# A short product of zeros in front of each float32r unit, and the g buffers at another distance from the weight slots

## The reference

```python
merged = g_s5 * (y_s5 @ w_br_s5[l]) + g_m * (y_m @ w_br_m[l])
x = x + merged @ w_out[l]
x = x + _cross_attn(h, _rmsnorm(mem, mem_norm_g[l]), x_wq[l], x_wkv[l], x_wo[l])
x = x + _conv_ffn(h, f_w_up[l], f_conv_w[l], f_conv_b[l], f_w_down[l])   # first block
...
y = even_mixer(...) if l % 2 == 0 else odd_mixer(...)                    # second block, twice
x = layer_norm(alpha * x + y, ln_g[l, 0], ln_b[l, 0])
y = conv_ffn(x, ffn_w_up[l], ffn_conv_w[l], ffn_conv_b[l], ffn_w_down[l])
x = layer_norm(alpha * x + y, ln_g[l, 1], ln_b[l, 1])
```

## Time and profile before

| | us |
|---|---|
| median of 3 runs | 1260.06 |
| lowest, highest | 1257.33, 1261.47 |
| profiled execution, its own time | 1257.58 |
| span of the profiled execution | 1256.3 |
| TensorE products busy | 1214.3 (97% of the span) |
| weight loads busy | 1115.8 (89%) |
| VectorE busy | 901.3 (72%) |
| ScalarE busy | 610.2 (49%) |

### The profile page before, as it was taken

One profiled execution on the slowest core, in us unless ns is written; L12 is line 12 of the kernel. 1 busy time (PEld: TensorE's weight loads), 2 busy tenths in 40 slices (PEclk: granted clock), 3 DMA queues, 4 the chain that ended last, 5 costly groups with the idle time before them and its releaser, 6 DMA issues. The chain is left out here.

```text
span 1256.3 us, 21189 instructions
## 1 busy us (share of the span) xinstructions
PE 1214.3 (97%) x8528; PEld 1115.8 (89%) x8528; DVE 901.3 (72%) x1266; ACT 610.2 (49%) x919; POOL 108.0 (9%) x148
## 2 busy tenths in 40 slices
PE   8999999989999999999998999999998999999997
PEld 5888888988999999989988899999986898999996
DVE  5977996574768888855678767767665689666677
ACT  2252213453656666644664545655414554655552
POOL 3893000003000000010000000000200000000000
PEclk9999999998999999999999999999999899999999
DMA  9543444535734766625425356667455205556560
GB/s 275 178 152 114 134 135 135 184 108 158 239 134 168 234 213 224 204 75 160 127 89 189 135 183 220 225 219 184 101 153 162 68 1 169 189 180 201 189 213 36
DMA packets 178734, 202.76 MB, mean 161 GB/s; under 512 B 21884, under 2 KB 163163, under 8 KB 178636
## 3 DMA queue, kind: packets, MB, share of 16 engines
q1 hardware_dynamic: 175083, 191.49, 47.9%
q0 software_dynamic: 3184, 9.77, 2.7%
q10 hardware_dynamic: 369, 0.13, 0.1%
HBM read 200.30 MB, written 1.08 MB: 160 GB/s over the span
## 5 line engine op out<-in xcount | busy, mean ns | idle before, releaser
L1483 DVE TENSOR_TENSOR w_parts<-raw,w_parts 128x1024 fp32r<-128x1024 f32 (+1 forms) x242 | 294.9, 1219 | 125.1 <-ACT w_parts L1472 119.8
L1766 PEld LDWEIGHTS ps<-hT_parts,w_parts 128*128 128x128 f32 x2880 | 338.5, 189 | 2.3
L1766 PE MATMUL ps<-hT_parts,w_parts 128*128 128x256 f32 x2880 | 340.3, 279 | 0.0
L1472 ACT CAST w_parts<-raw 128x1024 fp32r<-128x1024 f32 (+1 forms) x242 | 253.6, 1048 | 159.1 <-PE ps L1766 59.9
L478 PE MATMUL ps<-hT,ring 128*128 128x256 f32 x448 | 100.3, 384 | 1.2 <-DVE hT L321 1.2
L1536 PE MATMUL ps<-hT_parts,w_parts 128*128 128x256 f32 x816 | 98.5, 281 | 2.1 <-DVE w_parts L1483 1.5
L1536 PEld LDWEIGHTS ps<-hT_parts,w_parts 128*128 128x128 f32 x816 | 96.2, 189 | 2.9 <-DVE w_parts L1483 1.7
L478 PEld LDWEIGHTS ps<-hT,ring 128*128 128x128 f32 x448 | 85.7, 193 | 14.4 <-issue 1.6
L1890 DVE SCALAR_TENSOR_TENSOR arena_late<-ps,vecT,arena_late 128x255 f32<-128x255 f32 (+1 forms) x176 | 84.9, 482 | 10.3 <-ACT arena_late L1840 4.0
L1785 PE MATMUL ps<-w_parts,g0T_parts 128*128 128x512 f32 x360 | 86.7, 396 | 1.1 <-DVE w_parts L1483 1.1
L1785 PE MATMUL ps<-w_parts,g1T_parts 128*128 128x512 f32 x360 | 84.8, 390 | 0.0
(11 more groups left out here) (417 smaller groups left out, 1608.3 us busy)
## 6 DMA issues: line engine op xcount, KB each, us to landing
raw<-in_ffn_w_up SPq DMA_DIRECT2D x44, 1024.0 KB, 5.1
raw<-in_f_w_up SPq DMA_DIRECT2D x22, 1024.0 KB, 5.2
raw<-in_ffn_w_down SPq DMA_DIRECT2D x22, 1024.0 KB, 5.0
ring<-in_w_in SPq DMA_DIRECT2D x18, 1024.0 KB, 5.9
raw<-in_ev_w_in SPq DMA_DIRECT2D x15, 1024.0 KB, 5.4
raw<-in_f_w_down SPq DMA_DIRECT2D x11, 1024.0 KB, 5.0
ring<-in_x_wkv SPq DMA_DIRECT2D x8, 1024.0 KB, 5.4
ring<-in_w_out SPq DMA_DIRECT2D x4, 1024.0 KB, 8.2
```

Source lines behind the costliest of these rows:

```text
L1472: self.done(A, A.copy(high[:, c], self.raw[:, u % RAW, c]), self.s_hi)
L1483: self.done(V, V.tensor_tensor(low[:, c], self.raw[:, u % RAW, c], high[:, c].bitcast(F32), ALU.subtract), self.s_lo)
L1766: mm = T.matmul(self.ps[:, b, m * 256:m * 256 + 256], w[:, kk, m * P:(m + 1) * P], x[:, kk, :], start=kk == 0 and q == 0, stop=kk == KD - ...
```

## The change

Each unit of parts, and each PSUM bank of it where it has several, gets one product in front: 128 x 128 bfloat16 zeros as the stationary operand, 64 columns of zeros as the moving one. It writes columns 0 to 63 of the bank that the unit's first real product then overwrites. In `pe_up` a unit that is issued in two halves gets it before the first half alone. The pads around the g buffers change from 192 and 128 bytes to 320 and none: g0 moves up by 128 bytes, g1 and everything behind it stay where they are.

```diff
@@ pe_unit
             self.take(b)
+            if u in self.split1:
+                self.pe_short(b)
             for j in range(2):
@@ pe_out1
                 self.take(b)
+                self.pe_short(b)
                 for kk in range(KD):
@@
+    def pe_short(self, b):
+
+        self.T.matmul(self.ps[:, b, 0:64], self.zb[:, 0:P], self.zb[:, 0:64], start=True, stop=True)
@@ late_memory
-        for i, pad in enumerate((3, 2)):
-            self.sb(f"pad_g{i}", [P, pad * LINE])
+        for i, pad in enumerate((5, 0)):
+            if pad:
+                self.sb(f"pad_g{i}", [P, pad * LINE])
             self.gTr.append(self.sb(f"g{i}T_parts", [P, 2, 2, SEQ], F32R))
@@ pe_late
             self.take(b)
+            if split:
+                self.pe_short(b)
@@ pe_up
         self.take(b)
+        if half != 1:
+            self.pe_short(b)
```

## The result

| | before | after |
|---|---|---|
| median, us | 1260.76 (4 runs) | 1270.82 (4 runs) |
| lowest, highest | 1257.33, 1262.02 | 1267.6, 1272.37 |
| profiled execution: span | 1256.3 | 1269.5 |
| units with weights stationary, long pace | 2472 of 3936 products | 1368 of 3936 |
| units with weights moving, long pace | 735 of 864 | 492 of 864 |

The ratio is 1.0081 with a 95% interval of 1.0058 to 1.0103: 10 us slower, where the forecast was +0.2 us. The time lies inside the wide range (1251 to 1275) and outside the forecast's own (1256 to 1265). The last two rows of the table are counted from the timelines, stretch by stretch, in the way that the prediction counted.

A forecast was written before the change was run, and what follows sets the result against it. TensorE's stream of products was taken to bound the kernel: 13.1 us for zeros, less 11.0 from the pace and 1.9 from g0, made +0.2, put on the median as 1260.3 us; own range 1256 to 1265, wide range 1251 to 1275.

The forecast's parts named there:

- long pace: TensorE's 512-column products in some stretches: 118 ns from start to start, counted for 2472 of 3936 weights-stationary products.
- rival (a): All 118 starts: the zeros don't reset the pace, and units fall into the long pace; +17.7 us, 1277.8 us; chance 0.20.
- What bounds the kernel: Feed-forward networks: TensorE's products alone form the chain, so a nanosecond per product moves the end one for one.
- The price: All 118 products of zeros: 0.12 us each for an exposed weight load, less 1.1 us; 13.1 us, bounds 3.5 and 16.5.
- Rival (b): Products of zeros: cheap, only 0.03 us each, if loads could run two ahead; -9.4 us, 1250.7 us; chance 0.13.
- g0's move: Down units on g0: moving the buffer by 128 bytes brings 86.7 us to 84.8, worth 1.9 us.
- Nothing else differs: Down units on g0 against g1: position alone explains 86.7 against 84.8 us, so the move is worth 1.9 us.
- short pace: TensorE's 512-column products in the other stretches: 113 ns from start to start, counted for 1464 of 3936 weights-stationary products.
- The return: Weights-stationary units: all 2472 products at the long pace go to the short one, 11.0 us saved.
- 15 in 18 exposed starts: Weights-stationary units whose first weight load was exposed: 15 of 18 take the short pace, used to convert 2472 products.
- rival (c): Weights-moving units: another 735 products take the short pace too, 3.3 us; total -3.1 us, 1257.0 us; chance 0.17.
- The queues hold nothing new: DMA queues across the kernel: nothing else comes late, so they got no term in the sum.

## Why the prediction was right or wrong

The time fell into the wide range, but not for the reasons given. The forecast's own range ends at 1265, slower by more than 0.3% had a chance of 0.23, and the measured 1270.8 lies between the forecast and rival (a). Two things made the difference: the return was less than half of what was counted, and a stage that had no term in the sum grew. That the wide range covered the second one as well is luck.

**What bounds the kernel** held. In the networks each product of zeros is paid in full on the chain, and nothing hides it. No wait on VectorE appeared ahead of the up units.

**The price** held: 0.13 to 0.14 us for the 0.12 taken; 118 x 0.14 - 1.1 = 15.4 us at most for 13.1. The ground for it held too. The first real load begins with the product of zeros (both loads start together in the timeline of PEld, at 1104.03 and 1104.02, as the product of zeros does). Rival (b) is out, and the Trainium skill's issue floor of about 25 ns for products of up to 64 columns (TensorE: Matmul & The Clock Gate, Back-to-back issue gap) is not what such a product costs here. Beside float32r loads the first one costs 0.13 us; the second one in a row, at 0.03 to 0.04, is near it.

**g0's move** held in itself (1.6 us for 1.9), and failed in what it was taken to leave alone. The step "Nothing else differs" is wrong: a down unit at an odd multiple of 128 bytes gives the units behind it the short pace, and at a multiple of 256 the long one (but for the first down unit of a network, which leaves the long one in every trace without a second product of zeros). The prediction had this row before it (short pace behind g0 in 9 of 9 cases) and treated it only as a bound, on the ground that the zeros would reset the pace. In its trace the move alone costs 1.9 us in the networks.

**The return** is the step that failed: "every weights-stationary unit now begins behind a short product with a bare load", so all 2472 products would take the short pace. In net 1104 did: 1104 x 4.45 ns = 4.9 us for 11.0. 1152 of the remaining 1368 are 24 units, the first up unit behind each of the eight down units a network that have up units behind them. Fifteen of them had the long pace before and kept it; nine, behind g0, had the short one and lost it by the move of g0. There a single product of zeros changes nothing, as the experiment with zeros alone shows on both kinds of down unit; between two up units it does set the short pace. The count of 15 in 18 exposed starts came from starts behind transposes, attention groups and waits, with several short products or an idle array ahead; it was carried over to a single short product directly behind 512-column ones, of which the trace had no case. Behind down units two in a row suffice. Two readings on the way were off as well. The row of 11.26 us is no stretch at the short pace: (11.26 - 0.28)/95 is 115.6 ns, and the trace has 48 of its products at 118 and 48 at 113, with no break between. So a pace can change without one, and what changed it there is open. And that every stream behind products of 256 float32 columns starts at the long pace has an exception in the same trace: the unit at 607.33 stands behind eight of them and is 5.72 us long. Of the weights-moving units 243 products converted, 1.1 us, about a third of rival (c).

The sum of units by these terms: 15.4 - 4.9 - 1.1 - 1.6 + 0.3 = +8.1 us with every zero at 0.14, +5.8 at 0.12. By stages, 3.8 us are seen in the networks and 1.4 in the first block; what is left would stand in the mixers' stages, where the stretches at half clock differ between the two traces by more than that, so it is not shown. For the networks alone the terms are 60 x 0.13 - 576 x 4.45 ns - 1.6 + 0.3 = +3.9, against 3.8 measured. So rival (a), which wanted more than half of the 60 up units at the long pace, didn't come: 24 of 60 have it. The kernel lies between it and the forecast, and 0.21 us to win for 0.12 to pay was too thin a margin for a part of the units to miss it.

**What was not in the sum** is the stage at 292 us, +3.1 and +6.6 us in two profiled executions. "The queues hold nothing new" was wrong: instructions added to TensorE add code, and code comes through the same DMA engines. That the wait at the `x_wq` load goes with the position of the code is seen in both directions, in one trace each: 17 more products at the start bring it to the kernel before, 111 more take it from the changed one; and of twelve traces the four with a block in this load are the four with a wait of more than 1 us. The product of zeros itself does nothing there, since with two for one the wait is absent. What it costs the median is not shown. The kernel before with its code shifted has a ratio of 1.0019, about 2 us, and a median only 0.6 us up; the changed kernel with its code shifted on has nearly the ratio of the changed one. The shifted kernel's two clusters lie 4 to 5 us apart, but only an execution of the upper one was traced, and the kernel with two products of zeros has such an upper cluster without the wait. So of the 10 us the units account for 5 to 8, by the stages and by the terms; this stage, the start and the clock share the rest.

Not settled: why 16 KB cost a 1 MB load 1.3 to 4.5 us. The share of q1 in the 5.2 us from the issue is no proof, since it is 78.3% with the block and 79.9% without it in the kernel with its code shifted on, where the load is as fast as before the change. The block took 1.7 us of one DMA engine's time in the changed kernel's trace (2.1% of 16 engines in 5.2 us), and the copies of `bias_rows` begin right where the load should end; a part of the load that is held up by the block would then meet them at a third of the rate. No trace speaks against this, and it was not tested; a kernel that issues these copies later would do that.

## What to carry to other kernels

A stream of products has more than one pace, and what one unit ends with can set the pace of the next. So a position of a buffer is to be judged by the unit behind it too, not only by the products that read it: here 1.9 us won in the down units cost 3.8 in the up units. A count of cases (15 of 18) holds for the situation in which they were counted; before it is multiplied by a thousand products, look whether one of the cases is the one that the change makes. When instructions are added to TensorE, ask which load its code blocks will now meet. A stage whose trace grows by 3 to 5 us without any new dependence in it can be code.

## What the runs showed of the hardware

- **The pace and 256 bytes.** A 512-column float32r product with its load takes 227 ns when g (here the stationary operand) and the weight slots (here the moving one) are a multiple of 256 bytes apart (512 and 768), 232 ns at odd multiples of 128 (640 and 896), whichever buffer it is: down units of 5.44 to 5.46 and 5.57 us. The Trainium skill (TensorE: Matmul & The Clock Gate, Step-by-step) gives the array separate read ports for weights and moving data, and by that the position would be of no account. Four positions say otherwise. That it is a conflict of reads is not shown.
- **What resets the pace.** Directly behind a 512-column down unit one 64-column product of zeros leaves the pace that this unit set (24 of 24 places); two in a row put it to the short one (24 of 24). Between two up units one is enough (33 of 33 in the changed kernel's trace). For units with weights moving neither holds: 492 of 864 products stay at the long pace behind one. Why is not known.
- **Code blocks.** TensorE's code comes in blocks of 16 KB, 68 to 70 of them here, on queue q8. The Trainium skill (Runtime: NRT & Kernel Launch, Instruction fetch mechanics) says the same of the size and calls the cost mostly hidden. For TensorE itself the traces agree. For this load, which is due at once, they don't: 5.2 to 5.8 us without a block in it, 6.5 to 9.7 with one, in four profiled executions of twelve.
- **The clock.** Stretches at half clock stand in every kernel's trace, near 12 to 35, 283 to 297 and 962 to 1014 us, and their total, without the last one, in which the work ends, differs from one execution to the next: 20.5 us in the trace of before, 24 to 27 in most others, 31 to 34 in three. The first 17 us of before's trace are 1.6 to 2.2 us shorter than in eight of the others, 0.3 shorter than in one and 3.2 and 3.8 in two. Its profiled execution lies 2 to 4 us below the medians of its kind, so that single stages are not to be compared to a microsecond.
